# Expert weights fetched by halves of the contraction and multiplied in 512 columns; modulation weights fetched by 256 rows

## What is computed

```python
mod = split(silu(c) @ ada_w[l] + ada_b[l], 6)      # ada_w[l]: 1024 x 6144, the same map for c and c_ctx
p   = modulate(rms_norm(x), mod[0], mod[1]) @ w_in[l]
x   = x + mod[2] * (token_mixing(p) @ w_out[l])    # four head groups
h   = modulate(rms_norm(x), mod[3], mod[4])
# 16 experts, each token uses two of one group of four
hid = silu(h @ w_gate[e]) * (h @ w_up[e])          # w_gate, w_up: 1024 x 256
y   = sum_e (hid * gate[e]) @ w_down[e]            # w_down: 256 x 1024
x   = x + mod[5] * y
```

## Time and profile before

| | us |
|---|---|
| median of 3 runs | 888.6 (887.39 to 890.14) |
| span of the profiled execution | 884.8 |
| TensorE busy | 812.8 (92%) |
| VectorE busy | 550.0 (62%) |
| ScalarE busy | 468.4 (53%) |
| data moved by DMA | 198.01 MB, 224 GB/s on average |

### The profile page before, as it was taken

How to read it: one execution, slowest core, us unless ns; L and a number is a source line. 1 busy time by engine, 2 the same in 40 slices (tenths; PEclk the granted TensorE clock), 3 DMA queues, 4 the chain that set the end, 5 groups by cost and what they waited for, 6 DMA issues and landing times. The chain is left out here.

```text
span 884.8 us, 14943 instructions
## 1 busy us (share of the span) xinstructions
PE 812.8 (92%) x5938; PEld 685.0 (77%) x5938; DVE 550.0 (62%) x805; ACT 468.4 (53%) x652; POOL 79.2 (9%) x103
## 2 busy tenths in 40 slices
PE   3789999989999789999999957999999799999995
PEld 2368767756787689999999934798769589999994
DVE  2253323359632887777778646674395678978885
ACT  3263221268621755656666524763484466766763
POOL 0103000710004000000000031201300200000000
PEclk9789999999999699999999975999999889999998
DMA  9896898993212057889988869973063339999942
GB/s 323 261 291 151 278 313 270 311 318 118 63 50 94 1 175 246 288 296 302 303 289 288 270 220 347 262 226 125 17 222 111 96 100 308 349 335 349 341 170 74
DMA packets 169554, 198.01 MB, mean 224 GB/s; under 512 B 15586, under 2 KB 156428, under 8 KB 169484
## 3 DMA queue, kind: packets, MB, share of 16 engines
q1 hardware_dynamic: 165120, 183.06, 65.1%
q10 hardware_dynamic: 3212, 9.81, 2.9%
q0 software_dynamic: 1152, 4.19, 1.4%
HBM read 187.61 MB, written 9.44 MB: 223 GB/s over the span
## 5 line engine op out<-in xcount | busy, mean ns | idle before, releaser
L2231 DVE TENSOR_TENSOR w_lo<-raw,w_hi 128x2048 fp32r<-128x2048 f32 x96 | 219.6, 2290 | 32.1 <-ACT w_hi L1126 31.5
L1126 ACT ACTIVATE w_hi<-raw 128x2048 fp32r<-128x2048 f32 x96 | 183.6, 1913 | 64.1 <-PE bank L1263 55.1
L1261 PE MATMUL bank<-w_hi,xg_hi 128*128 128x256 f32 x384 | 111.7, 291 | 0.6 <-DVE xg_lo L2451 0.5
L1263 PE MATMUL bank<-w_hi,xg_lo 128*128 128x256 f32 x384 | 109.3, 285 | 0.0
L1262 PE MATMUL bank<-w_lo,xg_hi 128*128 128x256 f32 x384 | 109.2, 284 | 0.0
L1261 PE MATMUL bank<-h_hi,w_hi 128*128 128x512 f32 (+2 forms) x288 | 103.5, 359 | 6.1 <-DVE h_lo L1985 4.0
L1263 PE MATMUL bank<-h_hi,w_lo 128*128 128x512 f32 (+2 forms) x288 | 101.1, 351 | 0.0
L1262 PE MATMUL bank<-h_lo,w_hi 128*128 128x512 f32 (+2 forms) x288 | 101.1, 351 | 0.0
L1928 DVE TENSOR_TENSOR w_lo<-raw,w_hi 128x2048 fp32r<-128x2048 f32 (+1 forms) x20 | 45.3, 2267 | 50.3 <-ACT w_hi L865 50.1
L865 ACT ACTIVATE w_hi<-raw 128x2048 fp32r<-128x2048 f32 (+1 forms) x20 | 37.2, 1867 | 73.7 <-PE bank L1263 56.5
L1261 PEld LDWEIGHTS bank<-w_hi,xg_hi 128*128 128x128 f32 x384 | 74.2, 193 | 0.9 <-issue 0.9
(11 more groups left out here) (323 smaller groups left out, 1590.9 us busy)
## 6 DMA issues: line engine op xcount, KB each, us to landing
raw<-in_ada_w SPq DMA_DIRECT2D x46, 1024.0 KB, 10.0
raw<-in_moe_w_gate SPq DMA_DIRECT2D x32, 1024.0 KB, 6.7
raw<-in_moe_w_up SPq DMA_DIRECT2D x32, 1024.0 KB, 6.8
raw<-in_moe_w_down SPq DMA_DIRECT2D x32, 1024.0 KB, 6.2
raw<-in_w_in SPq DMA_DIRECT2D x14, 1024.0 KB, 11.4
raw<-in_w_out SPq DMA_DIRECT2D x8, 1024.0 KB, 7.1
y_rows<-y_sb ACTq DMA_DIRECT2D x16, 512.0 KB, 4.9
ada_first<-in_ada_w SPq DMA_DIRECT2D x2, 1024.0 KB, 12.5
```

The costliest lines, as they stand in the source:

```text
L1126: act.activation(w_hi[slot][:, :, :], raw[q][:, :, :], ACT.Copy).then_inc(split_hi, 1)
L1261: pe.matmul(dst, w_hi_, x_hi_, start=first, stop=False)
L1263: return pe.matmul(dst, w_lo_, x_hi_, start=False, stop=last)
L2231: dve.tensor_tensor(w_lo[slot][:, :, :], raw[q][:, :, :], w_hi[slot][:, :, :].bitcast(F32), ALU.subtract).then_inc(split_lo, 1)
```

## The change

1. A modulation block is now 256 rows x 1024 columns (4 KB runs). `wide` views a buffer as 2 x 1024; `modulate` waits for a block just before the two chunks of rows that it holds. Strips, matmul shapes and their number stay.
2. An expert's first two blocks are now the halves of the contraction: block 0 holds chunks 0 to 3 of gate and of up, block 1 chunks 4 to 7. A partition holds eight neighbouring rows (`(p k)` and no longer `(k p)`), so that chunk c is features 8p + c. Each expert block, the down block too, comes as two DMAs of 512 KB, on two semaphores (`loaded`, `loaded_b`).
3. Gate and up of one chunk are one product of 512 columns over the whole of bank 4: 24 matmuls of 512 columns in place of 48 of 256.
4. To fit, the gather reads every eighth feature of `h_tok` as its stationary operand (`features`), and its first run waits for all chunks of `h_tok` (`wait_copies`).
5. Semaphores are renamed and shared between the layers, the early blocks get their own; this is bookkeeping.

```diff
+        def landed(n):
+            if RAW <= n < RAW + EARLY:
+                return first_in[n - RAW], 16
+            return loaded[n % RAW], 16 * (n // RAW + (n < RAW or n % RAW >= EARLY))
+        def wide(block):
+            return block[:, :, :].rearrange("p (k g) n -> p k (g n)", k=2)
...
+        def features(rows, c):
+            return rows.rearrange("p (f k) -> p k f", k=KC)[:, c, :]
+        def gate_up(block, c):
+            return block[:, :, :].rearrange("p (r c) n -> p r c n", r=2)[:, :, c, :]
...
                 if r < N_ADA:
-                    src, c0, w = ada_w[bl], r * BW, BW
-                elif r < N_ADA + N_WIN:
+                    rows, cols = r % 4 * 2 * P, r // 4 * D
+                    sp.dma_start(wide(raw_of(bl, r)),
+                                 ada_w[bl][rows:rows + 2 * P, cols:cols + D].rearrange("(k p) n -> p k n", p=P)).then_inc(landed(n)[0], 16)
+                    return
...
-                        src = (w_gate, w_up, w_down)[role][l][bass.ds(2 * i + j, 1)]
-                        dst = raw[q][:, :, :]
-                        if role < 2:
-                            src = src.rearrange("a (k p) n -> p (a k) n", p=P)
-                        else:
-                            src = src.rearrange("a (f p) n -> p (a f) n", p=P)
-                            dst = dst.rearrange("p (f k) n -> p f (k n)", f=2)
-                        sp.dma_start(dst, src).then_inc(loaded[q], 16)
+                        for part, landed in enumerate((loaded[q], loaded_b[q])):
+                            dst = raw[q][:, 4 * part:4 * part + 4, :]
+                            if role < 2:
+                                src = (w_gate, w_up)[part][l][bass.ds(2 * i + j, 1)]
+                                src = src.rearrange("a (p k) n -> p (a k) n", k=KC)[:, 4 * role:4 * role + 4, :]
+                            else:
+                                src = w_down[l][bass.ds(2 * i + j, 1)].rearrange("a (f p) n -> p (a f) n", p=P)[:, part, :]
+                                dst = dst.rearrange("p k n -> p (k n)")
+                            sp.dma_start(dst, src).then_inc(landed, 16)
...
             def modulate(q, dst):
-                blocks = quad(q)
-                for l, j in blocks:
-                    n = raw_index(l, j)
-                    pe.wait_ge(loaded[n % RAW], 16 * (n // RAW + 1))
                 for k in range(KC):
-                    for g, (l, j) in enumerate(blocks):
-                        ins = pe.matmul(dst[32 * g:32 * g + 32, 0:BW], c_pad[:, k, :], raw_of(l, j)[:, k, :],
+                    l, j = quad(q)[k // 2]
+                    if k % 2 == 0:
+                        pe.wait_ge(*landed(raw_index(l, j)))
+                    for g in range(4):
+                        ins = pe.matmul(dst[32 * g:32 * g + 32, 0:BW], c_pad[:, k, :], wide(raw_of(l, j))[:, k % 2, g * BW:(g + 1) * BW],
                                         start=(k == 0), stop=(k == KC - 1))
...
                 def wait_copies(part, half, l=l):
-                    if part == 0:
-                        pe.wait_ge(q_ta, l * KC + 4 * (half + 1))
-                    else:
-                        pe.wait_ge(q_td, l * KC + (8 if half else 6))
+                    pe.wait_ge((q_ta, q_td)[part], (l + 1) * KC)
...
                                     ins = pe.matmul(bank[c // 2][:, (c % 2) * 2 * SLOTS:(c % 2 + 1) * 2 * SLOTS],
-                                                    h_tok[part][:, t, c * P:(c + 1) * P], onehot[:, t, :],
+                                                    features(h_tok[part][:, t, :], c), onehot[:, t, :],
...
-                                for c in range(KC):
-                                    if even and role == 0 and c % 4 == 0:
-                                        pe.wait_ge(x_hi, 2 * i + (m * E + 2))
-                                        pe.wait_ge(x_lo, 2 * i + (m * E + c // 4 + 1))
+                                if even:
+                                    pe.wait_ge(x_hi, 2 * i + (m * E + 2))
+                                    pe.wait_ge(x_lo, 2 * i + (m * E + role + 1))
+                                for c in range(4 * role, 4 * role + 4):
                                     sl = slice((j % 2) * SLOTS, (j % 2 + 1) * SLOTS)
-                                    ins = product(bank[4][:, role * FE:(role + 1) * FE], xg_hi[:, c, sl], xg_lo[:, c, sl],
-                                                  w_hi[role][:, c, :], w_lo[role][:, c, :], c == 0, c == KC - 1)
+                                    ins = product(gate_and_up, xg_hi[:, c, sl], xg_lo[:, c, sl],
+                                                  gate_up(w_hi[role], c % 4), gate_up(w_lo[role], c % 4), c == 0, c == KC - 1)
```

More of the change, by code:

```diff
@@ L286, in build @@
         loaded = [sem(f"loaded{i}") for i in range(RAW)]
+        loaded_b = [sem(f"loaded_b{i}") for i in range(RAW)]
+        first_in = [sem(f"first_in{i}") for i in range(EARLY)]
         s_ident = sem("s_ident")
@@ L358, in raw_of @@
             n = raw_index(l, r)
-            return ada_first[n - RAW] if RAW <= n < 8 else raw[n % RAW]
+            return ada_first[n - RAW] if RAW <= n < RAW + EARLY else raw[n % RAW]
+        def landed(n):
[4 more added lines that the diff above has]
+            return block[:, :, :].rearrange("p (k g) n -> p k (g n)", k=2)
         def quad(q):
@@ L1205, in dense_round @@
                             for half in range(2):
-                                act.wait_ge(d_ghi, 4 * k + 2 * e + half + 1)
+                                act.wait_ge(g_hi, DENSE + 4 * k + 2 * e + half + 1)
                                 for b in range(2):
@@ L1802, in gather @@
                             if part == 1:
-                                pe.wait_ge(d_xhi, 4 * k + 2 * i + half + 1)
+                                pe.wait_ge(x_hi, DENSE + 4 * k + 2 * i + half + 1)
                             elif i == 1:
-                                pe.wait_ge(d_xlo, 4 * k + half + 1)
+                                pe.wait_ge(x_lo, DENSE + 4 * k + half + 1)
                             for c in range(4 * half, 4 * half + 4):
@@ L1808, in gather @@
                                     ins = pe.matmul(bank[c // 2][:, (c % 2) * 2 * SLOTS:(c % 2 + 1) * 2 * SLOTS],
-                                                    h_tok[part][:, t, c * P:(c + 1) * P],
+                                                    features(h_tok[part][:, t, :], c),
                                                     onehot_g[:, t, 2 * i * SLOTS:(2 * i + 2) * SLOTS],
                                                     start=(t == 0), stop=(t == nt - 1))
-                            ins.then_inc((d_ghi, d_glo)[part], 1)
-                    pe.wait_ge(d_p, k + 1)
+                            ins.then_inc((g_hi, g_lo)[part], 1)
+                    pe.wait_ge(q_p, DENSE // 2 + k + 1)
                     if k:
@@ L1854, in dense_round @@
                                 if role == 0:
-                                    pe.wait_ge(d_m, k * E + e)
-                                for c in range(KC):
-                                    if e % 8 == 0 and role == 0 and c % 4 == 0:
-                                        pe.wait_ge(d_xhi, 4 * k + e // 4 + 2)
-                                        pe.wait_ge(d_xlo, 4 * k + e // 4 + c // 4 + 1)
+                                    pe.wait_ge(q_m, DENSE + k * E + e)
+                                if e % 8 == 0:
+                                    pe.wait_ge(x_hi, DENSE + 4 * k + e // 4 + 2)
+                                    pe.wait_ge(x_lo, DENSE + 4 * k + e // 4 + role + 1)
+                                for c in range(4 * role, 4 * role + 4):
                                     i, sl = e // 8, slice((e // 4 % 2) * SLOTS, (e // 4 % 2 + 1) * SLOTS)
-                                    ins = product(bank[4][:, role * FE:(role + 1) * FE], pair_hi[i][:, c, sl], pair_lo[i][:, c, sl],
-                                                  w_hi[role][:, c, :], w_lo[role][:, c, :], c == 0, c == KC - 1)
+                                    ins = product(gate_and_up, pair_hi[i][:, c, sl], pair_lo[i][:, c, sl],
+                                                  gate_up(w_hi[role], c % 4), gate_up(w_lo[role], c % 4), c == 0, c == KC - 1)
                                 ins.then_inc(used, 1)
@@ L2448, in dense_round @@
                             for half in range(2):
-                                dve.wait_ge(d_glo, 4 * k + 2 * e + half + 1)
+                                dve.wait_ge(g_lo, DENSE + 4 * k + 2 * e + half + 1)
                                 for b in range(2):
@@ L2452, in dense_round @@
                                                           bank[2 * half + b][:, :])
-                                ins.then_inc(d_xlo, 1)
+                                ins.then_inc(x_lo, 1)
                             if k == 0 and e == 0:
```

56 lines of the change are left out of this document (31 added, 25 removed).

## The result

The changed kernel takes 944.0 us (median of 4 executions, 943.39 to 944.66) against 888.0 for the kernel before beside it: 1.062 of its time, 95% interval 1.060 to 1.065, slower by 56 us. The profiled execution spans 942.1 us, 57.3 more than before.

What follows compares the result with a forecast made beforehand. TensorE, busy 92% of the span, was taken as the bound. Terms 6.4 + 3.2 + 1.8 - 0.3 = 11.1 us off the 884.8 us span gave 873.7, plus 3.8 around it 877.5 us; range 867 to 890.

Steps and rivals of the forecast that it cites:

- The strided gather: Gathers in both layers: reading `h_tok` weights at a step of 8 elements costs nothing, loads staying hidden under matmuls.
- The sign named for it: Gathers: weight loads of `h_tok` listed at over 215 ns would show the forecast wrong; 190 ns would show it right.
- The rival with the doubled column: Gathers: a strided weight column takes twice 0.84 ns, 576 x 0.096 = 55 us more, 932.8 us; chance 0.17.
- Gate and up in 512 columns: Experts: 24 matmuls for 48 save 0.20 us an expert, 6.4 us in all; bounds nothing and 13.1 us.
- The start: Before the first projection: 4 KB modulation rows at 395 GB/s bring `nh` and TensorE's first projection 3.2 us earlier.
- The step named as next late: Start: ScalarE splits projection block 1 ahead of `nh`; its earlier landing lets `nh` start 3.2 us earlier.
- its upper end of 4.2 us: Start: the most it could gain, with modulation blocks arriving at 417 GB/s.
- The quad in the attention: Attention: TensorE's 1.76 us wait before the modulation quad goes whole, at either load rate; counted as 1.8 us.
- First gather: Layer 0: the first gather run waits for the last copy of `h_tok`, losing 0.3 us; nothing in layer 1.
- The expert loads: Experts: two DMAs per block add 1.1 us of issue per expert, hidden; nothing waits for long even with 1 KB packets.
- A wait of TensorE for `w_lo` among the experts: Experts: TensorE was to stay busy throughout; its waiting for `w_lo` or a DMA would show the forecast wrong.

Runs made afterwards that it cites:

- steps 4, 8 and 16: Changed kernel with the gather's stationary operand read every 4 elements (938.8 us), every 8 (the change itself, 944.0) or every 16 over two token tiles (932.7).
- step 2: Changed kernel with the gather's stationary operand read every 2 elements (8 bytes), expert rows permuted to match: 879.2 us, ratio 0.988.
- the run with the waits ahead: Against the changed kernel with `h_tok` written in gather order: all four waits of a modulation quad put before its first matmul; 879.9 us, ratio 0.988.
- the kernel written in order: Changed kernel, but features are permuted when `h_tok` is written, so gathers read 128 neighbouring words; 877.7 us, ratio 0.987.
- the modulation alone: Changed kernel with experts computed as before (48 products of 256 columns, 1 KB rows, neighbouring features), only modulation blocks new; 883.5 us, ratio 0.994.
- four other kernels: Changed kernel with `h_tok` written in gather order, plus gate/up moving operand at step 4 (1050.0 us) or 8 (1025.7), strided gate/up weights (892.3), quad waits first (879.9).

## Why the prediction was wrong

- **The strided gather: the step that failed.** It was costed at nothing, because the moving operand gets a word every 0.44 ns and a column of weights only every 0.84 ns, so that a path at half speed would still be in time. It measured 66.4 us in the trace, 67.4 in the kernel before with this edit alone. The argument took one operand's rate for the capacity of the other's path. Both paths halve with one word per 16 bytes, each from its own rate: the moving one from 0.45 to 0.90 ns, the weights to 0.237 / 128 = 1.85 ns a column. There was no reserve of a factor of two in the weight path, and the estimate from the trace had said so: a load of 108 ns under a spacing of 118. The sign named for it, weight loads of `h_tok` over 215 ns, came with 337.
- **The rival with the doubled column** had the right mechanism and place. Its 0.096 per matmul measured 0.119, so it gave 932.8 where 944.0 came. Its size came from the difference of two listed loads, (190 - 136) / 64 = 0.84 ns a column, where half of the measured 1.85 is 0.93; how long a load of neighbouring words takes by itself no run shows. It deserved more than 0.17, since the only row against it was of the other operand. The Trainium skill's rule on lines of 16 bytes (SBUF — State Buffer, section Door 1: The DMA port swizzle) stood beside this rival; the runs bear it out, steps 4, 8 and 16 paying and step 2 not.
- **Gate and up in 512 columns**: 0.20 us an expert forecast, 5.55 against 5.84 measured, 0.29. Without the stalls of the strided kernel the sum over all experts falls from 192.3 to 184.4, 7.9 us for 6.4, inside the bounds. The two pieces of 256 columns cost nothing that shows: 5.55 us for 24 matmuls, 5.64 in the projection.
- **The start**: 3.2 us forecast, 3.6 measured, at some 410 GB/s where 395 was taken. The step named as next late, projection block 1 with swap and split ahead of `nh`, was the right one, and the run with the waits ahead shows that the rate and not the waits sets it. Two slips of the prediction move nothing: its upper end of 4.2 us should read 4.3 (4.0 + 0.3), and slices 11 to 34 of the earlier trace rows hold 345, 352 and 357 beside the 347 to 350 that it reads there. The Trainium skill's rule (DMA: Bandwidth & Descriptors, section Specifications) that transfers from 512 B reach line rate does not hold here: rows of 1 KB came at 347 to 349 GB/s and rows of 4 KB at 397 to 422.
- **The quad in the attention**: the 1.76 us went, as forecast. At the first matmul of the output projection TensorE is 4.6 us ahead (237.66 to 233.10), less than 5.0 + 0.4: the first projection's 192 matmuls took 36.75 us for 35.98. They took 35.89 in the kernel written in order and 35.96 with the modulation alone, so this 0.8 us belongs to the one trace and not to the change.
- **First gather**: 0.3 us forecast. TensorE waits 0.8 us there, and of the 4.6 us ahead 3.35 are left. In the kernel written in order its 64 matmuls then took 10.23 us for 8.41, a term that the sum did not have; the granted clock reads 0.50 from 301 to 306 us there. As the 8.88 to 10.17 us of the same matmuls in four other kernels show, up to 1.4 us of this goes with the moment at which the full clock came back.
- **The expert loads** were costed at nothing and cost nothing that shows; that TensorE bounds them at 1 KB too was right. A wait of TensorE for `w_lo` among the experts, named as a sign of being wrong, did come, 1.2 us in all, with either length of rows. Why is open.

Without the stride the other terms hold in kind: they said 11.1 us less, 877.5, and the kernel that keeps everything but the stride took 877.7, 12.1 us less than the kernel before beside it and 9.8 in the trace. That it is this close is in part luck: gate and up brought 1.5 us more than forecast, and the first gathers took 1.8 us that were not in the sum.

## What to carry to other kernels

Price the access pattern of a stationary operand by itself: in fp32, from a step of 16 bytes on, a load of 128 columns takes 0.22 to 0.24 us, twice the 0.118 in which a matmul of 256 columns had just covered it, and every such matmul waits. If a layout must be permuted, do it where the tile is written once (here a copy out of PSUM, for nothing) and not where it is read 576 times. And when a cost is argued away by another path's speed, look for the margin in the path itself first; a load estimated at 108 ns under 118 has hardly any.

## What the runs showed of the hardware

- A step of 4 elements or more halves the rate of both operands of TensorE in fp32: with strided weights a matmul of 256 columns starts every 0.219 to 0.237 us in place of 0.118, with a moving operand at step 4 a word takes 0.90 ns in place of 0.45. A step of 2 costs 2% (weights). A step of 16 is slightly cheaper than one of 8 (0.219 for 0.237).
- Under matmuls of 512 columns a strided load costs 0.022 us instead of 0.12.
- ScalarE and VectorE read PSUM with a step of 8 elements at the speed of neighbouring words (588 and 682 ns for 512 elements, 592 and 683 with neighbouring words).
- Modulation blocks in rows of 4 KB arrived at 397 to 422 GB/s, in rows of 1 KB at 347 to 349.
- After a half idle stretch at half clock, the full clock came back 3 us after the first gather of layer 1 in one trace and 13 us after it in another, in front of the same work, worth 3.8 us here. A wait of 1.8 us in mid-stream was followed by 1.7 us of lower clock in one trace and by none in two. A gain of a few us ahead of such a place may not arrive at the end.
